# Convolution to merge of a two-block network: zero rows written earlier, three modulation pieces ahead of the first gate, a semaphore per row slot, scores in f16 parts, the merge by token halves

## The reference

```python
# first block: a convolution module, then a mixture of 32 experts, 2 for each token
mod = silu(c) @ ada_w + ada_b                       # sh1, sc1, g1, sh2, sc2, g2
h = rmsnorm(x, norm_mix_g) * (1 + sc1) + sh1
u = h @ conv_w_in + conv_b_in; a, gt = split(u, 2); u = a * sigmoid(gt)
y = depthwise_conv31(u) + conv_b_dw
y = silu(layernorm(y, conv_ln_g, conv_ln_b)) @ conv_w_out
x = x + g1 * y
h = rmsnorm(x, norm_ffn_g) * (1 + sc2) + sh2
x = x + g2 * hier_moe(h, ...)                       # rows gathered by expert; an empty slot counts zero
# second block: 8-head attention on the 256 keys of highest index score, and an SSM branch
sc = einsum("bthd,bshd->bths", q, k) * 128 ** -0.5  # masked to the kept causal keys
y_att = (softmax(sc) @ v * silu(z_att)) @ w_branch_att
merged = sigmoid(g_att) * y_att + sigmoid(g_ssm) * y_ssm
x = x + gate * (merged @ w_out)
```

## Time and profile before

| | us |
|---|---|
| median of 3 executions | 2813.41 (2810.64 to 2813.62) |
| profiled execution, own time | 2811.98 |
| its span, first to last instruction | 2810.2 |
| PE busy | 2524.1 (90%) |
| DVE busy | 1633.0 (58%) |
| ACT busy | 980.7 (35%) |
| POOL busy | 597.8 (21%) |
| mean granted PE clock, share of full | 0.951 |

### The profile page before, as it was taken

One profiled execution on the slowest core, in us unless ns is written; L12 is line 12 of the kernel. 1 busy time (PEld: TensorE's weight loads), 2 busy tenths in 40 slices (PEclk: granted clock), 3 DMA queues, 4 the chain that ended last, 5 costly groups with the idle time before them and its releaser, 6 DMA issues. The chain is left out here.

```text
span 2810.2 us, 39777 instructions
## 1 busy us (share of the span) xinstructions
PE 2524.1 (90%) x15471; PEld 1356.5 (48%) x15471; DVE 1633.0 (58%) x2912; ACT 980.7 (35%) x1512; POOL 597.8 (21%) x489
## 2 busy tenths in 40 slices
PE   4999984989799996798899989998999999999978
PEld 3555543545455553354334447743454444444433
DVE  5788565222223334576499976544775757747842
ACT  6111452121122223564542335421543524615510
POOL 1011021000000001331432200000540722703613
PEclk8999986999999998899899989999999999999999
DMA  9555868699999997220112300053002002020051
GB/s 242 185 175 160 278 247 311 234 387 385 398 378 362 386 342 267 79 68 8 45 38 90 105 23 1 12 207 127 8 1 98 8 10 89 9 90 8 1 222 78
DMA packets 129229, 433.05 MB, mean 154 GB/s; under 512 B 27760, under 2 KB 37360, under 8 KB 120752
## 3 DMA queue, kind: packets, MB, share of 16 engines
q1 hardware_dynamic: 97680, 359.10, 34.9%
q10 hardware_dynamic: 21216, 38.97, 4.0%
q0 software_dynamic: 10176, 32.78, 3.8%
HBM read 371.86 MB, written 58.94 MB: 153 GB/s over the span
## 5 line engine op out<-in xcount | busy, mean ns | idle before, releaser
L1381 PE MATMUL m_gu<-conv_y,m_xT 128*64 128x256 f32 x1024 | 234.4, 388 | 17.4 <-DMA arena<-in_moe_w_up 15.1
L1383 PE MATMUL m_gu<-arena,m_xT 128*64 128x256 f32 x1024 | 234.4, 389 | 0.0
L2448 POOL TENSOR_TENSOR group_words<-group_words 128x1024 f16<-128x1024 f16 x64 | 149.8, 2362 | 373.6 <-PE i_pj L142 364.4
L1460 DVE TENSOR_TENSOR m_hid<-m_sg,m_gu 64x256 f32<-64x256 f32 x96 | 39.7, 413 | 324.0 <-ACT m_sg L1429 324.0
L1383 PEld LDWEIGHTS m_gu<-arena,m_xT 128*64 128x64 f32 x1024 | 143.4, 141 | 72.0 <-issue 15.3
L1403 PE MATMUL m_y_ps<-arena,m_hidT 128*64 128x512 f32 x768 | 175.4, 598 | 0.0
L1429 ACT ACT_TABLE_LOAD x48 | 61.6, 1283 | 304.3 <-issue 291.7
L1381 PEld LDWEIGHTS m_gu<-conv_y,m_xT 128*64 128x64 f32 x1024 | 143.4, 140 | 35.6 <-issue 25.3
L140 PE MATMUL i_pj<-hT,group_words 128*128 128x512 f16 x384 | 146.5, 382 | 13.3 <-DVE group_words L322 7.9
L140 PE MATMUL s_pj<-hT,arena 128*128 128x512 f16 x384 | 149.7, 390 | 0.0
L141 PE MATMUL s_pj<-hT,arena 128*128 128x512 f16 x384 | 149.4, 389 | 0.0
(11 more groups left out here) (544 smaller groups left out, 6415.1 us busy)
## 6 DMA issues: line engine op xcount, KB each, us to landing
arena<-in_moe_w_down SPq DMA_DIRECT2D x32, 2048.0 KB, 23.5
conv_y<-in_moe_w_gate SPq DMA_DIRECT2D x22, 2048.0 KB
arena<-in_moe_w_up SPq DMA_DIRECT2D x22, 2048.0 KB
hT<-in_moe_w_gate SPq DMA_DIRECT2D x10, 2048.0 KB
hT<-in_moe_w_up SPq DMA_DIRECT2D x10, 2048.0 KB
x_tok<-in_ada_w ACTq DMA_DIRECT2D x7, 2048.0 KB, 12.3
slot_out<-m_y ACTq DMA_DIRECT2D x96, 128.0 KB
arena<-in_w_gates SPq DMA_DIRECT2D x24, 512.0 KB, 4.1
```

The lines of the kernel that those rows point to most:

```text
L1381: g = nc.tensor.matmul(gu_ps[i][g_rows, 0:FFN // 2], lhsT=xT[:, c, :], rhs=k.wg[e % WEIGHT_SLOTS][:, c, cols], start=c == 0, stop=c == KC - 1)
L1383: u = nc.tensor.matmul(gu_ps[i][u_rows, 0:FFN // 2], lhsT=xT[:, c, :], rhs=k.wu[e % WEIGHT_SLOTS][:, c, cols], start=c == 0, stop=c == KC - 1)
L1460: nc.vector.tensor_tensor(hid[:, i, :], sg[:, i, :], gu_ps[i][u_rows, 0:FFN // 2], ALU.mult) \
L2448: return tuple(k.nc.gpsimd.tensor_tensor(k.y_U[:, t % 2, n], k.adt_parts[:, n, t, heads].unsqueeze(2).to_broadcast([P, HPG, P]), k.upto16. ...
```

## The change

1. **Zero fill.** Four DMAs of 2 MB go on ACT's queue in iterations 1 to 4 of `conv_stage`, behind the weights and the piece of that iteration, from a tile of zeros of its own (512 columns, so each element is 2 KB where it was 4 KB). `front_stage` has none of it.
2. **Pieces.** `conv_stage` takes pieces 4 to 11, the eighth behind its last evacuation; PE waits for one piece at a time. `front_stage` has pieces 12 to 15 and does three of them (was two) ahead of `gate_rows(0)`. The first is loaded into the second half of `x_tok` right behind the projection weights; `x` comes in two halves.
3. **Row slots.** `row_root` writes its squares elsewhere, and `normalise(t)` waits for the last store of its own slot, with four semaphores in place of one.
4. **Scores in f16.** In the select stage ten more ACT copies and ten more POOL subtractions split q (8 blocks) and k (2 heads); the scores are three f16 matmuls in place of an f32 one.
5. **Merge.** The gate product, the sum, its high and low part go by halves of 512 tokens; the low part is DVE's; PE's first four tiles wait for the first half only. The last tile is done by column halves, its residual addition on DVE, with two output DMAs.

```diff
@@ pieces
-FIRST_PIECES, SECOND_PIECES, THIRD_PIECES, GATE_PIECES = (2, 3, 0, 1), range(4, 11), range(11, 16), (16, 17)
+FIRST_PIECES, SECOND_PIECES, THIRD_PIECES, GATE_PIECES = (2, 3, 0, 1), range(4, 12), range(12, 16), (16, 17)
@@ conv_stage, tensor
-            pe.wait_ge(ada_used, len(SECOND_PIECES))
             for n, j in enumerate(SECOND_PIECES):
+                pe.wait_ge(ada_used, n + 1)
                 modulation_sums(k, k.late_ps[:, 0, 0:72], sums[:, n, :], j)
@@ conv_stage, scalar
                 if i < len(SECOND_PIECES):
                     ada(i)
+                if 1 <= i <= ZERO_PARTS:
+                    act.wait_ge(zero_sb, 1)
+                    zero_fill(k, act, i - 1, zeros[:, :], zeroed)
+            act.wait_ge(zeroed, 16 * ZERO_PARTS)
             last_half(act, 1)
@@ front_stage, vector
-            for n in range(2):
+            for n in range(3):
                 for part in range(2):
                     piece(n, part)
             gate_rows(0)
@@ front_stage, scalar
             def row_root(t):
-                slot = normed[:, t % 4, :]
                 act.wait_ge(added, t + 1)
                 if t == 0:
-                    act.wait_ge(low, KC)
-                    act.wait_ge(ada_used, 2)
+                    act.wait_ge(sq_used, 2 * KC)
...
-                if t >= 4:
-                    act.wait_ge(k.normed_stored, 16 * t)
-                    act.wait_ge(turned, 2 * (t - 3))
-                nc.scalar.activation(slot, k.x_tok[:, t, :], ACT.Square, accum_out=ss[:, t:t + 1]).then_inc(row_squared, 1)
+                if t:
+                    act.wait_ge(row_squared, t)
+                nc.scalar.activation(junk, k.x_tok[:, t, :], ACT.Square, accum_out=ss[:, t:t + 1]).then_inc(row_squared, 1)
...
             def normalise(t):
                 act.wait_ge(row_rstd, t + 1)
+                if t == 0:
+                    act.wait_ge(low, KC)
+                    act.wait_ge(ada_used, 3)
+                if t >= 4:
+                    act.wait_ge(k.normed_stored[t % 4], 16 * (t // 4))
+                    act.wait_ge(turned, 2 * (t - 3))
@@ select_stage, gpsimd
+                    n = j - first_part
+                    if 0 <= n < len(k.whole):
+                        pool.wait_ge(part_high, n + 1)
+                        nc.gpsimd.tensor_tensor(k.parts[n][:, 1, :], k.whole[n], k.parts[n][:, 0, :], ALU.subtract) \
+                            .then_inc(part_low, 1)
@@ attention_stage, tensor
-                    last = nc.tensor.matmul(s_ps[m % 2][:, a:e], lhsT=k.qT[:, b, h, :],
-                                            rhs=k.kT[:, h // (HEADS // KV_HEADS), a:e], start=True, stop=True)
+                    last = product(nc, s_ps[m % 2][:, a:e], part(q_parts(b), slice(h * P, (h + 1) * P)),
+                                   part(k_parts(h), slice(a, e)), True, True)
@@ merge_out_stage, tensor
-                pe.wait_ge(m_high, c + 1)
-                pe.wait_ge(m_low, c + 1)
+                pe.wait_ge(m_high, 2 * c + 1)
+                pe.wait_ge(m_low, 2 * c + 1)
@@ merge_out_stage, vector
             for c in range(KC):
...
+                for h in range(2):
+                    s, a = sig[:, c % 4, cols(h)], att[:, c % 4, cols(h)]
+                    dve.wait_ge(sig_in[c % 4], 16 * (c // 4 + 1))
+                    nc.vector.tensor_tensor(s, s, k.y_ssm[:, c, cols(h)], ALU.mult).then_inc(mul, 1)
+                    dve.wait_ge(mul, 2 * c + h + 1)
+                    dve.wait_ge(att_in[c % 4], 16 * (c // 4 + 1))
+                    nc.vector.tensor_tensor(a, a, s, ALU.add).then_inc(summed, 1)
+                    if c == h == 0:
+                        split(0)
+                        merged_low(0, 0)
+                if c:
+                    merged_low(c, 0)
                 if c + 1 < KC:
                     split(c + 1)
+                merged_low(c, 1)
```

More of the change, by code:

```diff
@@ L78, in row_constants, with zero_fill @@
         .astype(np.float32)
[L81 to L89, removed]
+ZERO_PARTS = 4
+def zero_fill(k, eng, i, zeros, done):
+    first = 2 * S // P
+    n = (SLOT_BLOCKS * BLOCK // P - first) // ZERO_PARTS
+    a = (first + i * n) * P
+    eng.dma_start(k.slot_out[a:a + n * P, :].rearrange("r (h d) -> (r h) d", d=HALF).rearrange("(b p) d -> p b d", p=P),
+                  zeros.unsqueeze(1).to_broadcast([P, 2 * n, HALF])).then_inc(done, 16)
 class Core:
@@ L782, in _ @@
             turn(2)
-            for n in range(3):
+            for n in range(4):
                 late_sums(n)
@@ L2999, in _, with products @@
             last.then_inc(gate_mm, 1)
-            def products(t, c):
-                for h in range(2):
-                    last = product(nc, acc[t % 4][:, h * HALF:(h + 1) * HALF],
-                                   part(merged, c, slice(t * P, (t + 1) * P)),
-                                   part(ws, c, slice(h * HALF, (h + 1) * HALF)), c == 0, c == KC - 1)
+            def products(t, c, halves=range(2)):
+                for h in halves:
+                    last = product(nc, acc[t % 4][:, cols(h)], part(merged, c, slice(t * P, (t + 1) * P)),
+                                   part(ws, c, cols(h)), c == 0, c == KC - 1)
                 return last
@@ L3022, in _, with weight_high @@
                 last.then_inc(mm_done, 1)
+            pe.wait_ge(gated_done, TT - 4)
+            for h in range(2):
+                for c in range(KC):
+                    last = products(TT - 1, c, (h,))
+                last.then_inc(mm_done, 1)
         @block.scalar
         def _(act):
+            def weight_high(c):
+                act.wait_ge(w_in[c], 16)
+                high_part(nc, ws[:, 0, c, :], w[:, c % 4, :]).then_inc(high, 1)
+            weight_high(0)
             act.wait_ge(gate_mm, 1)
@@ L3120, in mixer_program @@
             k.qT = k.x_tok[:, :, :].rearrange("p t (h q) -> p t h q", q=P)
+            spare = 2 * UNIT + sum(P * (b + 1) for b in range(TOPK // P, TT))
+            k.whole = [k.x_tok[:, t, :] for t in range(TT)] + [k.kT[:, a, :] for a in range(KV_HEADS)]
+            k.parts = [x.bitcast(F16).rearrange("p (a n) -> p a n", a=2)
+                       for x in [cells(k, spare + n * S, S) for n in range(2)] + k.whole[:-2]]
             tokens_stage(k)
```

153 lines of the change are left out of this document (84 added, 69 removed).

## The result

| | before | after |
|---|---|---|
| median, us | 2812.02 (4 runs) | 2780.10 (4 runs, 2774.43 to 2785.64) |
| ratio of the first comparison | | 0.9888 (95%: 0.9865 to 0.9911) |
| ratio of the second (5 runs after) | | 0.9897 (95%: 0.9879 to 0.9916) |
| profiled span | 2810.2 | 2777.6 |

One execution of the last kernel of experiment 9 took 2860.51 us at a mean granted clock of 0.908; all others, of every kernel, were at 0.951 or more, and ratios use these alone.

A forecast was written before the change was run, and what follows sets the result against it. PE was taken as the bound, stage by stage, with waits in the front stage and merge. Terms of -18.2, +1.0, +3, -0.5, -2, -9.4 and -14.6 sum to -40.7 us: 2771.3 profiled, 2773 as median, range 2764 to 2786.

The forecast's parts named there:

- The front gap: Front stage: PE's 13.4 us stop before tile 3 goes whole, with 1.3 us of slow clock behind it: 14.7 us.
- My -18.2: Front stage in total: 14.7 us from the gap and 3.5 from the row slots, between -12 and -20.
- The row slots: Front stage, row 7: ACT no longer waits for an earlier row's store, -3.5 us, or 0 if row 3's store is late.
- +4.0: Convolution in total: +1.0 us for the eighth piece and +3 for the zeros.
- Zeros +3: Convolution, four iterations: zeros delay the cu_parts store by 7 to 8.4 us against 7 of slack, +3 us, bounds 0 and +10.
- Eighth piece +1.0: End of the convolution: PE sums eight pieces instead of seven, 1.03 us more, with its DVE work hidden.
- if its load came 2.1 us late: End of the convolution: the eighth piece's DVE work is hidden unless its load is 2.1 us late, costing from there on.
- -2 expected: Select stage: most DVE decisions fall free of POOL's added subtractions, -2 us, bounds -2.9 and +21.
- The rival of +21: Select stage: POOL holds DVE for 2.13 us ten times, +21 us instead of -2, giving 2796 us; chance 0.08.
- Attention: Attention scores as f16 matmuls: the pace per job falls by 0.07 to 0.43 us in blocks 4 to 7, -9.4 us.
- Merge: Merge: PE becomes the bound at 5.17 us a chunk, was 6.75, -12.4; halves at the end -2.2; total -14.6 us.

The follow-up runs named there:

- last kernel of experiment 9: Changed kernel with seven pieces in the convolution, the eighth back in the front stage, and two of the seven sums ahead of the last taps: median 2778.25 us, ratio 0.9878.
- experiment 4: Changed kernel with the old rule for row slots put back, a row's square waiting for the stores of all slots: 2785.54 us, one run.
- experiment 2: Changed kernel with twice the zeros, 2 MB more in each of convolution iterations 1 to 4: 2784.32 us, one run.
- experiment 1: Changed kernel with the load of the eighth late piece issued only when the last store to conv_u has landed: 2777.79 us, one run.
- 6: Changed kernel with the eighth late piece loaded only when the last loads of cu_ph have landed: 2782.77 us, one run.
- 9: Changed kernel with the eighth piece back in the front stage, seven in the convolution: 2769.76 us, ratio 0.9854; the changed kernel again beside it: 2784.48 us.
- experiment 7: Changed kernel with the low parts of the merge back on POOL, by halves: 2788.34 us, one run.
- experiment 3: Changed kernel with the PE sums of two of the eight pieces ahead of the last taps: 2775.60 us in one run, later 2774.86 us, ratio 0.9866.

## Why the prediction was right, and where it was not

**The front gap: right, the last microsecond by luck.** It went whole. Tile 3 starts 14.8 us earlier against the stage's start: 13.4 for the gap, and 1.4 because PE's first tiles met a faster clock (0.89 in the ten us in which it was 0.75), which I had not foreseen. The 1.3 us of slow clock behind the gap came on top. But the rows were not ready sooner by as much: PE's wait before the first transposes grew from 0.64 to 1.98, and these too start 14.8 earlier, where I had 14.7. In seven of twelve traces the clock fell behind it and behind the late sums: the first transposes took 1.49 us for 0.93, 24 matmuls 6.29 for 5.18, the sums 4.82 for 3.49, 24 more with router logits 7.77 for 5.78, 5.0 us in all. In the five others it did not, nor at 410, where the kernel before had 0.67; there the front was 20 to 21 us shorter than before. My -18.2 lies between the two kinds, and no term of mine tells them apart.

**The row slots: right in size, wrong in cause.** From the transposes of row 6 to those of row 7 PE took 10.57 us and now takes 7.06, the 3.5 less that I had. But with the old rule put back (experiment 4) it takes 7.06 as well, so in the new order this gain does not come from the rule: it goes with the other order of loads. I had kept the stores' delays as they were. What the rule does save is 7 us at row 4, against fronts at full clock, and that I had at nothing.

**The convolution's terms: both wrong, and their sum near by luck.** I had +4.0 for +5.7. "Zeros +3" was 0. I had them delay the store of `cu_parts` by 7 to 8.4 us; in iterations 1 to 4 the loads are issued 7.4 to 9.2 us behind the store, where it was 7.8 to 8.5, and PE never waits. By experiment 2 twice as much costs 2.5. "Eighth piece +1.0" measured at least 5.6. It failed in the words "if its load came 2.1 us late": I asked when the piece lands, not what stands behind it. The trace of before had the number, 2.7 us against 8.0 for the store of the one iteration without a piece in front. Six traces with the convolution as in the change gave tails of 33.3 to 36.2 (27.7 before, 27.8 without the piece), so it costs 5.6 to 8.5. Of 5.6 in the first trace 1.7 is the later start of the taps and 3.9 are the sums. Four pieces take 3.49 us at full clock in the front, 0.9 each; my 1.03 was a mean that had slow clock in it. So one more piece is 0.9 of the 3.9, and the rest is clock: it falls at 293 to 294 in both kernels, when about one piece was left before and five are left now. In the longer tails the last taps run slow as well, 8.3 us for 6.8. Moving the load moved the collision (experiments 1, 6), and taking the piece out removed it (9).

**Select: wrong mechanism.** I let DVE's decisions slip past POOL's moved window. They did once, and then the second subtraction caught the next instruction, and DVE was held at the same phase as ever, by the end of the last subtraction. This is why the stage did not move at all in this trace (-2 expected), and became no shorter than 273.3 us in any with the added work. The Trainium skill, SBUF — State Buffer, section "Who interferes with whom", counts an operation of DVE with two SBUF inputs among those that wait for GpSimd's reads; line 2147 has them, and the trace agrees, with 2.04 us for 0.16. The rival of +21 came true only when a third subtraction stood in the burst: +18.3.

**Attention: right, but for the split over the blocks.** Jobs of block 7 take 3.96 (3.95 expected). By the starts of DVE's masks, block 4 gave nothing (0.6 expected) and block 5 0.1 (2.4): there DVE already ran at 2.99 us a job although PE needs 3.28, because PE had come in with a lead from the blocks before. Blocks 6 and 7 gave 3.7 and 4.6 for the 3.0 and 3.4 that I had. Over the stage it is 8.6 for 9.4.

**Merge: right,** 14.8 for 14.6, chunks at PE's 5.17, DVE at 4.99 for the 5.0 that I took. By experiment 7 both the halves and the move to DVE were needed.

**Branch and SSM, +1.8,** was in no term. In its first 34 us, in halves, PE's clock was 0.76 and 0.94 where it was 0.80 and 1.00, which is 1.7 us of full clock. In all traces of changed kernels this stretch, to the last SSM operation, took 825.7 to 827.3 us, 825.2 before. Why the clock is lower there no run tested.

## What to carry to other kernels

Where a load is moved into a busy stage, ask what else is on its way at that time, not only whether it lands in time: 2 MB beside a 512 KB store on the path cost 5.6 to 8.5 us where its sums take 0.9 at full clock, while 8 MB in iterations with slack cost nothing. A stall between two engines that run in rhythm is not the sum of its collisions: it can be a lock that more work leaves nearly alone, until the burst is long enough to catch a second instruction. Work that PE's slow clock makes dear should not stand last in a stage where it sets the end (experiment 3); where something else sets the end, moving it gives nothing (the last kernel of 9). And a gain of the forecast size can come from another part of the change: undo the parts one by one.

## What was not expected of the hardware

- The same order of work and the same idle time of 1.98 us was followed by a fall of the granted clock in seven traces and by full clock in five; in experiment 4 the clock stayed full behind it too and fell only behind the longer stop. Windows of 10 us of experiment 1, at full clock, where the changed kernel shows 0.83 and 0.66 above:

```profile
380.00:390.00 10.00, 8.02 (x42) 3.98 (x41) 6.01 (x12) 9.50 (x11) 4.42 (x3) 1.00 0.52 179
...
400.00:410.00 10.00, 10.00 (x88) 7.25 (x87) 3.57 (x7) 5.94 (x9) 2.93 (x2) 1.00 1.02 422
```

- 2 MB of zeros from 512-column rows beside 5.3 million other bytes took the DMA share only from 0.61 to 0.83, where I had 0.92; doubled, 0.93 to 0.98 with 339 to 352 GB/s, more than the 270 GB/s that I had read off the front stage and took for the rate of the zeros.
